# Where TensorE decides on further rounds: in front of the last three expert pairs, written out in both arms, or behind the last scatter

## The reference, cut to what matters

```python
def moe_ffn(h, w_router, b_router, w_gate, b_gate, w_up, b_up, w_down, b_down):
    logits = (h @ w_router + b_router).astype(jnp.float32)
    top_val, top_idx = lax.top_k(logits, TOP_K)
    gates = jax.nn.softmax(top_val, axis=-1).astype(h.dtype)
    ...
    def expert_block(args):
        xb, e = args
        g = xb @ w_gate[e] + b_gate[e]
        u = xb @ w_up[e] + b_up[e]
        g = jnp.minimum(g, SWIGLU_LIMIT)
        u = jnp.clip(u, -SWIGLU_LIMIT, SWIGLU_LIMIT)
        glu = g * jax.nn.sigmoid(SWIGLU_ALPHA * g)
        return ((u + 1.0) * glu) @ w_down[e] + b_down[e]
```

## Time and profile before

| | us |
|---|---|
| median of the three runs | 1101.59 |
| the profiled execution | 1101.59 |
| its span, from the first to the last instruction | 1099.8 |
| PE busy in the span | 1045.9 (95%) |
| mean transfer rate over the span | 398 GB/s |
| mean granted clock of TensorE | 0.986 of full speed |

### The profile page before, as it was taken

One profiled execution on the slowest core, in us unless ns is written; L12 is line 12 of the kernel. 1 busy time (PEld: TensorE's weight loads), 2 busy tenths in 40 slices (PEclk: granted clock), 3 DMA queues, 4 the chain that ended last, 5 costly groups with the idle time before them and its releaser, 6 DMA issues.

```text
span 1099.8 us, 12728 instructions
## 1 busy us (share of the span) xinstructions
PE 1045.9 (95%) x5458; PEld 503.6 (46%) x5458; DVE 302.7 (28%) x622; ACT 130.9 (12%) x243; POOL 13.1 (1%) x18
## 2 busy tenths in 40 slices
PE   9999999999999999999899989999799989999896
PEld 8999996534433443344234423433243324343332
DVE  5977888420302121121112111030202011212022
ACT  2212250310000001001000010000000100000012
POOL 1200000000000000000000000000000000000000
PEclk9999999999999999999899999999899989999999
DMA  9974377999999999999999999999999999999996
GB/s 337 427 295 154 138 296 295 352 428 428 434 430 440 431 436 431 434 436 434 427 441 431 434 434 431 436 431 431 436 434 427 443 429 421 434 429 430 425 428 250
DMA packets 22771, 438.24 MB, mean 398 GB/s; under 512 B 4560, under 2 KB 5968, under 8 KB 9424
## 3 DMA queue, kind: packets, MB, share of 16 engines
q1 hardware_dynamic: 22160, 435.05, 93.2%
q10 hardware_dynamic: 576, 2.69, 0.6%
HBM read 436.28 MB, written 1.05 MB: 398 GB/s over the span
## 4 chain that ended last, share of the span: by engine, by line
PE 62%; DMA 35%; DVE 1%; issue 1%; ACT 1%; DVEq 0%; SPq 0%; POOL 0%; POOLq 0%
DMA ring<-in_experts 35%; PE ps L2133 26%; PE ps L2182 11%; PE ps L1688 8%; PE ps L2039 3%; PE ps L2191 2%; PE ps L1867 2%; PE ps L1683 2%; PE ps L1932 2%; PE ps L1737 1%; PE ps L2171 1%; PE ps L2048 1%; PE ps L2149 0%; ACT region_va L911 0%; PE ps L1809 0%
## 5 line engine op out<-in xcount | busy, mean ns | idle before, releaser
L2133 PE MATMUL ps<-ring,xT 128*64 128x512 f32 x2044 | 461.2, 607 | 26.1 <-DMA ring<-in_experts 26.1
L2133 PEld LDWEIGHTS ps<-ring,xT 128*64 128x64 f32 x2044 | 145.3, 139 | 314.2 <-issue 285.3
L2182 PE MATMUL ps<-ring,region_va 128*64 128x512 f32 x1024 | 227.2, 595 | 18.8 <-DMA ring<-in_experts 11.1
L2182 PEld LDWEIGHTS ps<-ring,region_va 128*64 128x64 f32 x1024 | 73.5, 137 | 150.9 <-issue 138.0
L1583 DVE TENSOR_SCALAR g<-ps 128x1024 f32<-128x1024 f32 x16 | 19.6, 1225 | 349.1 <-PE ps L2133 343.2
L1688 PE MATMUL ps<-ring 128*128 128x128 f32 x784 | 89.7, 276 | 0.1
L1688 PEld LDWEIGHTS ps<-ring 128*128 128x128 f32 x784 | 88.5, 192 | 0.9 <-DVE ring L997 0.3
L1605 DVE TENSOR_SCALAR region_va<-ps 128x512 f32<-128x512 f32 x32 | 22.1, 692 | 183.0 <-PE ps L2133 183.0
L1529 DVE TENSOR_TENSOR xT<-ps,g_ffn 128x512 f32<-128x512 f32 x30 | 20.7, 692 | 187.0 <-PE ps L2039 187.0
L2039 PEld LDWEIGHTS ps<-sel,x 128*128 128x128 f32 x480 | 55.4, 192 | 9.5 <-issue 9.5
L2191 PE MATMUL ps<-g,g_T 128*128 128x512 f32 x128 | 59.2, 605 | 0.0
(11 more groups left out here) (271 smaller groups left out, 548.3 us busy)
## 6 DMA issues: line engine op xcount, KB each, us to landing
ring<-in_experts SPq DMA_DIRECT2D x19, 4096.0 KB, 40.6
ring<-in_experts SPq DMA_DIRECT2D x28, 2048.0 KB, 12.4
ring<-in_head SPq DMA_DIRECT2D x13, 2048.0 KB, 15.8
ring<-in_experts SPq DMA_DIRECT2D x12, 1024.0 KB, 8.5
ring<-in_experts SPq DMA_DIRECT2D x7, 512.0 KB, 8.1
ring<-in_first SPq DMA_DIRECT2D x7, 384.0 KB, 6.9
ring<-in_experts ACTq DMA_DIRECT2D x2, 1024.0 KB, 9.1
ring<-in_experts SPq DMA_DIRECT2D x1, 1536.0 KB, 6.5
```

Source lines behind the costliest of these rows:

```text
L2133: last = mm(bank(banks + half)[rows, :], xT[:, 2 * m + c, rows], weights[:, k], start=False, stop=m == 3 and c == 1, skip_group_check=True)
L2182: last = mm(bank(first + half)[rows, :], hTm[:, 2 * m + c, rows], w[:, c, half, k], start=m == 0 and c == 0, stop=m == 3 and c == 1, skip_ ...
```

## The change

TensorE loads the number of rounds and branches on it right behind the loop, in front of pair 13. The last three pairs stand twice in its program, once in each arm. In the arm for more than one round they are followed by the further gather and the further loops; in the other arm they stand alone, behind all of that. The other engines keep their decision where it was. Their programs are the same, instruction for instruction.

```diff
-            for n in range(WHOLE_PAIRS + 1, PAIRS - 1):
-                expert_pair(n, n % PAIRS_PER_ITER)
-            expert_pair(PAIRS - 1, 1, last_pair=True)
+            def closing_pairs():
+
+                for n in range(WHOLE_PAIRS + 1, PAIRS - 1):
+                    expert_pair(n, n % PAIRS_PER_ITER)
+                expert_pair(PAIRS - 1, 1, last_pair=True)
+
             def gather_again():
 
                 pe.wait_ge(sel_ready, PAIRS + 1)
                 gather(pair_bank(1), range(KC))
 
-            rounds_after_first(pe, expert_iteration, resume=gather_again)
+            pe.wait_ge(nr_ready, 1)
+            rounds = pe.value_load(nr_i[0:1, 0:1], min_val=1, max_val=ROUNDS)
+            with pe.If(rounds > 1):
+                closing_pairs()
+                gather_again()
+                with pe.Fori(1, rounds) as r:
+                    with pe.Fori(0, ITERS) as i:
+                        expert_iteration(i, r * ITERS + i)
+            with pe.Else():
+                closing_pairs()
```

## The result

The changed kernel took 1103.81 us, the median of eight runs (1102.36 to 1106.82). Before took 1101.64 us beside it. The ratio is 1.0027, with a 95% interval of 1.0018 to 1.0037, so the change costs 2.0 to 4.1 us. (One execution of before took 1209.19 us, a slow one, and the ratio leaves it out.) Run again beside the experiments it gave 1103.99 us against 1101.37, ratio 1.0026 (1.0017 to 1.0035). The forecast was 1102.7: the direction came as written, and so did each kind of step on the way, a stall on a fetch, a fall of the clock and waits that fill part of both. The cost is two to three times the +1.1 us, because the stall is longer. The profiled execution after took 1102.36 us with a span of 1100.6, the lowest of its runs.

A forecast was written before the change was run, and what follows sets the result against it. The prediction took weight loading to bound the kernel. Idle PE of 3.4 us plus 3.1 us lost to the clock, less 5.38 us of waits filled, gave +1.1 us on 1101.59: 1102.7 us, range 1101.0 to 1106.0.

The forecast's parts named there:

- the +1.1 us: At the kernel's end: net delay forecast, 6.5 us of PE delay less 5.38 us of waits that it fills.
- What bounds the kernel: Expert stage: bound by loading weights; PE's waits in the last three pairs can make up 5.38 us of delay.
- Load, compare and lead of the sequencer: In front of pair 13: load and compare take 0.9 us; the sequencer is 1.8 us ahead of PE.
- The jump stalls: In front of pair 13: the jump over the written-out pairs needs an instruction fetch; branch 3.74 us before any wait behind weights.
- How long it stalls: In front of pair 13: 2.8 us plus 0.6 behind weights, 3.4 us of idle PE, ends 2.8 and 9.3.
- the fetch's wait behind the weights: At the jump before pair 13: fetch waits for the packet being moved, 0 to 1.25 us, 0.6 taken.
- the prediction's own test: In front of pair 13: the prediction counts as wrong if PE's idle time is over 4.5 us.
- The wider end of the range: At the jump before pair 13: upper end for the fetch beside loads, up to 6.5 us more.
- The rival of the fetch behind a whole share: Before pair 13: fetch waits for an engine's whole load share, 5 us mean; idle 7.8 us, 1107.1 us; chance 0.17.
- What the clock costs: Behind the stall: the clock falls to half speed and PE loses 3.1 us, lower end 0.
- The reading that 3.4 us lies just on the side where the clock fell: Behind the stall: loop waits of 3.21 and 4.78 us dropped the clock, so 3.4 us of idle would too.
- The end: Behind the last scatter: removing load, compare, branch and fetches is worth 0, with a bound of 1.2 us gained.

The follow-up runs named there:

- front_of_15: Changed kernel with the decision moved to in front of pair 15, pairs 13 and 14 being common code; 1107.78 us against 1101.14, ratio 1.0059.
- hot_arm_first: Changed kernel with its two arms swapped, so the common case falls through in front of pair 13 and jumps at the end; 1101.26 us, ratio 0.9997.
- short_jump: Kernel before plus a second load of the number and a branch over a single wait in front of pair 13; 1101.46 us, ratio 1.0.
- load_at_end: Changed kernel with arms swapped, plus the number loaded once more behind the three pairs of the arm that runs; 1101.88 us.
- thin_loads: Changed kernel with the loads of the last three pairs cut to 64 columns per piece, most weights left out; 1100.40 us, one execution.
- before_look: Kernel before repeated without an edit, for a second profile of its tail; 1100.78 us.
- load_early: Kernel before with the number loaded in front of pair 13 and the branch left at the end; 1101.25 us, ratio 1.0.
- behind_gate: Changed kernel with pair 13's gate product issued in common code ahead of the decision; 1101.47 us, ratio 0.9999.
- again: Changed kernel repeated without an edit; 1103.99 us, median of eleven runs.
- again_look: Changed kernel repeated once more without an edit, for a further sample of branch and clock; one execution at 1103.97 us.
- two_pairs_earlier: Changed kernel with the loop cut to five turns, the decision in front of pair 11 and pairs 11 to 15 in both arms; 1102.05 us, ratio 1.0007.

## Why the prediction was right in direction and too small

- **What bounds the kernel: right.** Loads bound it, PE had time to spare in the last three pairs, and a delay beyond that reaches the end. Against the trace that was read 5.25 us was given back, where 5.38 was written; over six traces the spare time is 3.1 to 5.9 us, so that one trace came so near the account is partly luck. It lies a little otherwise than written: of the 2.04 us at 1018.62 in the earlier trace rows 0.77 remain, for ACT, and pair 15 gives 0.7 in place of 0.37. front_of_15 shows the other half: with only those 0.7 us of waits behind the stall, 6.5 of 7.2 us is paid.
- **Load, compare and lead of the sequencer: right.** 0.8 to 0.9 us and 1.8 us; hot_arm_first and short_jump, which have these alone, cost nothing.
- **The jump stalls: right.** A near jump takes 0.2 us and one over the written-out pairs needs a fetch, as read from the earlier trace rows. The Trainium skill says the same in "Runtime: NRT & Kernel Launch", section "Instruction fetch mechanics": a taken branch whose target lies outside the window of fetched pages stops until its page is there. The traces agree, with 0.22 us against 3.3 to 7.2; it gives no duration.
- **How long it stalls: the step that failed.** The prediction took "0 to 1.25 us, 0.6 in the mean" for the fetch's wait behind the weights, half a packet on one engine. The far jumps without weights took 3.28 (load_at_end), 3.36 (thin_loads), 3.38 (before_look), 3.60 (short_jump, at its end), 3.74 (before), 3.83 and 3.83 us (load_early, hot_arm_first). Those among weights took 5.90, 6.08, 6.30, 6.53, 6.86 and 7.20. The means are 3.57 and 6.48: the weights add 2.9 us, not 0.6, and idle PE is 4.9 to 5.9 us, not 3.4. By the prediction's own test (wrong over 4.5 us) this step fell. The wait does lie in front of the packet, as the prediction had it, but it is 2.3 to 3.6 us longer there, not half a packet of 32 KB. The wider end of the range, up to 6.5 us more, held. A cost of over 0.2%, which a ratio of 1.0027 is, had been given a chance of 0.28.
- **The rival of the fetch behind a whole share: wrong in size too.** It asked for 7.8 us of idle PE and 1107.1. Six jumps gave 4.9 to 6.2 of idle, or 3.0 with the longer lead. The extra wait was 2.3 to 3.6 us in every sample (each less the mean of 3.57), where this rival had 5 in the mean and 10 at most. Both prices lay beside the truth, one below and one above. So the rule that the Trainium skill has in "DMA: Bandwidth & Descriptors", section "Queues, rings and completion order", is not borne out as I priced it.
- **What the clock costs: right in kind, too large in the mean.** 3.1 us was taken from two stretches in which PE worked almost throughout. The losses are 1.5, 1.7 and 2.9, since part of the slow stretch can fall on the idle time, or be only 3.4 us long. By luck this error of -1.1 hid half of the stall's +2.1. The reading that 3.4 us lies just on the side where the clock fell came from too few waits. In before the clock stayed at 1.00 around a wait of 2.04 us and the product took 3.65 us; in before_look, the same kernel, it was 0.50 from 1019.0 to 1022.4 behind the same wait, and the product took 5.35. Just ahead of it PE had waited 1.09 us in before and 1.95 in before_look.

```profile
1018.68 5.35 PE L2182 MATMUL ps<-ring,region_va 128*64 128x512 f32 x16 [2.04 <-DMA ring<-in_experts]
```

- **The end: 0 taken, bound of 1.2 gained.** At most 0.55 us in some executions. behind_gate and load_early show no gain that the timing can tell, and no version with all its weights beats the kernel before.

In the sum, with means over the three profiles: 5.48 of stall and 2.03 of clock, less 5.25, is 2.3 us, where 3.4 + 3.1 - 5.38 was written. The term that was mis-sized is the wait of the fetch among the weights.

## What to carry to other kernels

Price a jump by where its target is and by what the transfer engines do at that moment: with the common case falling through in front of pair 13, the far jump stood at the end and cost nothing here. A stall in a stage with spare time costs only what the waits behind it can't fill, so read those waits one by one, and look for what releases the same instruction next, before a cost is called hidden. A price taken from a quiet place in the trace didn't hold in a busy one; no row showed the busy case, and the measured 2.9 us lay near the middle of the range of 0 to 6.5, not near its quiet end. Spare time read from one trace is one sample: here it was 3.1 to 5.9 us.

## What the runs showed of the hardware

- A far jump on PE's sequencer took 3.3 to 3.8 us with no weights beside it and 5.9 to 7.2 us among weights at 414 to 438 GB/s. The addition is 2.7 us among 16 KB packets, 2.3 to 3.3 among 32 KB and 3.6 among 64 KB, with one sample each of the first and the last: it does not grow with the packet in proportion. All of it lies in front of the instruction packet. What the packet waits for in these 2 to 4 us stays open.
- A jump that is taken to a near target takes 0.2 us, one that falls through 0.07 to 0.08.
- How far the sequencer runs ahead of PE differed with what is queued: 1.8 us behind the gather's 128x128 products, 4.4 us behind the 128x512 ones (behind_gate, one sample).
- After a stop of 5 to 6 us the granted clock was 0.50 for 3.4 us in one execution (again) and for 6.6 to 6.8 us in four (after, again_look, front_of_15, two_pairs_earlier). After the 3.02 us of behind_gate it was 0.50 for 3.3 us. How much of that stretch lay on idle time, and how long it was, decided the loss.
- A wait of 2.04 us left the clock at 1.00 in before and came with 0.50 in before_look: the length of the last wait alone does not decide.
